# Second input projection in a two-block layer: 46 instead of 34 gate units computed beside the expert gather, and shorter filling steps behind it

## The reference

```python
# first block
z = rmsnorm(x, norm1_g) @ w_in
merged = gates[:, :, 0] * conformer_conv(conv_in) + gates[:, :, 1] * (windowed_gqa(q, k, v) @ attn_w_o)
x = x + merged @ w_out
x = x + peer_ffn(rmsnorm(x, norm2_g))
x = rmsnorm(x, final_g)
# peer_ffn, per token: 8 heads x 16 experts
u, vv = expert_u[expert_idx], expert_v[expert_idx]
out = sum(gate * gelu(u . h) * vv)
# second block
p = rms_norm(x, norm_g) @ w_in_2
y_a = rwkv7_mix(p_r, p_k, p_v, p_w, p_a) * silu(z_a)
y_b = sliding_window_sink_attn(p_q, p_sk, p_sv) * silu(z_b)
y_c = memory_cross_attn(p_xq, mem) * silu(z_c)
gates = sigmoid(p_gate)          # 3 x 1024 columns
merged = gates[0] * (y_a @ w_proj_a) + gates[1] * (y_b @ w_proj_b) + gates[2] * (y_c @ w_proj_c)
x = x + merged @ w_out
```

## Time and profile before

| | |
|---|---|
| median of three runs | 2453.41 us (2452.80 to 2457.09) |
| the profiled execution | 2445.02 us |
| its span | 2443.2 us |
| TensorE busy in matmuls | 2156.0 us, 88% |
| TensorE weight loads (beside them) | 1428.3 us, 58% |
| VectorE | 1756.2 us, 72% |
| ScalarE | 849.9 us, 35% |
| POOL | 698.8 us, 29% |
| DMA, mean | 291 GB/s |
| TensorE's granted clock | 0.983 of full |

### The profile page before, as it was taken

How to read it: one execution, slowest core, us unless ns; L and a number is a source line. 1 busy time by engine, 2 the same in 40 slices (tenths; PEclk the granted TensorE clock), 3 DMA queues, 4 the chain that set the end, 5 groups by cost and what they waited for, 6 DMA issues and landing times. The chain is left out here.

```text
span 2443.2 us, 34816 instructions
## 1 busy us (share of the span) xinstructions
PE 2156.0 (88%) x12550; PEld 1428.3 (58%) x12550; DVE 1756.2 (72%) x3976; ACT 849.9 (35%) x1966; POOL 698.8 (29%) x580
## 2 busy tenths in 40 slices
PE   8999899998989898877777887789888898999999
PEld 7887566764444444422323333367766788867677
DVE  7999796587767667677777676798887546466763
ACT  4222664243323232223333233433333232225641
POOL 0001312354333333333443333334233000011133
PEclk9999999999999999999999999999999999998999
DMA  4333214599999999999999999999999653232152
GB/s 155 104 104 112 78 53 165 180 395 415 421 420 414 415 419 416 411 416 418 409 420 413 410 419 420 399 413 416 420 398 408 227 188 116 83 126 106 40 194 95
DMA packets 135482, 710.39 MB, mean 291 GB/s; under 512 B 14480, under 2 KB 23568, under 8 KB 69520
## 3 DMA queue, kind: packets, MB, share of 16 engines
q0 software_dynamic: 73728, 536.90, 53.3%
q1 hardware_dynamic: 61584, 171.26, 19.8%
HBM read 686.61 MB, written 21.50 MB: 290 GB/s over the span
## 5 line engine op out<-in xcount | busy, mean ns | idle before, releaser
L2176 PE MATMUL bank<-peer_uv,peer_diag 128*128 128x512 f32 x1856 | 875.3, 614 | 221.9 <-ACT peer_diag L1549 211.1
L1915 DVE SCALAR_TENSOR_TENSOR peer_uv<-peer_uv,h 128x1024 f32<-128x1024 f32 x512 | 618.5, 1219 | 323.8 <-DMA peer_uv<-in_peer_uv,peer_index 321.8
L1596 POOL DMA_INDIRECT peer_uv<-in_peer_uv,peer_index x512 | 536.5, 1048 | 858.6 <-PE bank L2176 599.4
L2176 PEld LDWEIGHTS bank<-peer_uv,peer_diag 128*128 128x128 f32 x1856 | 339.9, 193 | 664.2 <-issue 663.8
L168 PE MATMUL bank<-hT_high,weight_low 128*128 128x512 f32 (+1 forms) x952 | 348.4, 366 | 0.0
L166 PE MATMUL bank<-hT_high,weight_high 128*128 128x512 f32 (+1 forms) x768 | 333.9, 435 | 8.1 <-PEq L454 2.4
L240 POOL TENSOR_TENSOR weight_low<-weight_ring,weight_high 128x1024 fp32r<-128x1024 f32 x52 | 127.4, 2451 | 613.3 <-ACT weight_high L223 613.3
L167 PE MATMUL bank<-hT_low,weight_high 128*128 128x512 f32 (+1 forms) x768 | 285.3, 371 | 1.2 <-issue 1.2
L1542 ACT ACTIVATE peer_gelu<-peer_dots 128x2 f32<-128x2 f32 (+1 forms) x257 | 52.0, 202 | 646.4 <-DVE peer_uv L1915 646.0
L223 ACT ACTIVATE weight_high<-weight_ring 128x1024 fp32r<-128x1024 f32 x148 | 156.2, 1055 | 307.0 <-PE bank L168 297.6
L1549 ACT ACTIVATE peer_diag<-const,peer_weight 128x128 f32<-128x128 f32 x464 | 163.7, 395 | 226.3 <-DVE peer_weight L1711 223.6
(11 more groups left out here) (468 smaller groups left out, 3141.6 us busy)
## 6 DMA issues: line engine op xcount, KB each, us to landing
weight_ring<-in_weights SPq DMA_DIRECT2D x218, 512.0 KB
z_store<-fill_stage SPq DMA_DIRECT2D x36, 256.0 KB, 2.3
peer_uv<-in_peer_uv,peer_index POOLq DMA_INDIRECT x512, 11.8
z_store<-early_stage SPq DMA_DIRECT2D x34, 192.0 KB
merge_z<-z_store SPq DMA_DIRECT2D x8, 768.0 KB, 6.8
merge_z<-z_store SPq DMA_DIRECT2D x12, 512.0 KB, 4.7
raw_query<-in_weights SPq DMA_DIRECT2D x10, 512.0 KB, 6.7
raw_out<-in_weights SPq DMA_DIRECT2D x8, 512.0 KB, 7.0
```

The costliest lines, as they stand in the source:

```text
L1596: pool.indirect_dma_start(uv[:, p % SLOTS], None, peer_uv, bass.IndirectOffsetOnAxis(index[:, n % 2, p % TOPK:p % TOPK + 1], 0)).then_inc( ...
L1915: nc.vector.scalar_tensor_tensor(uv[:, p % SLOTS, 0:D], uv[:, p % SLOTS, 0:D], 1.0, h2[:, t], ALU.mult, ALU.mult, accum_out=dots[:, p % TO ...
L2176: mm = nc.tensor.matmul(bank[2 * t + c][:], diag[:, p % SLOTS], uv[:, p % SLOTS, D + c * 512:D + (c + 1) * 512], start=(n == first_of(t) a ...
```

## The change

`EARLY` goes from 34 to 46, so all gate units are computed beside the gather for 384 tokens. The units begin three groups sooner (group 204 instead of 207), for which the norm of a complete tile is drawn together from 16 groups to 12: its last step on VectorE stood 15 groups after `FINISH_AT`, now 12, and TensorE's turn stood at 9, now at 6. Two instead of three units are left behind the last group, and the copy behind the warm-up Sqrt falls away. A third buffer for the copies lies in the place of a score table. The wait for all stores moves from the end of SP's program in this block to ScalarE's in `rwkv_prepare`. VectorE may make two low parts in one group. Behind the gather all fill steps are short ones now, 46 x 4 = 184, and the blocks from the chain of states on hold fewer: 7 instead of 14 in the chain, 12 instead of 24 in the outputs (the 3 steps behind the last output become 1), 11 instead of 18 in the finishing block, 18 instead of 38 in the windowed attention, none instead of 2 in the merge. Up to the end of the solve they are 136, as before.

```diff
@@ constants
-EARLY = 34
+EARLY = 46
+STAGES = 3
@@ class Weights
+        self.early_stored = [ctx.enter_context(nc.semaphore(f"early_stored{i}")) for i in range(STAGES)]
...
+    def wait_early_stored(self, eng):
+
+        for i in range(STAGES):
+            eng.wait_ge(self.early_stored[i], 16 * ((EARLY + STAGES - 1 - i) // STAGES))
@@ places beside the gather
-FINISH_DVE = (2, 4, 6, 8, 9, 12, 13, 14, 15)
-FINISH_ACT = (3, 5, 7, 10, 11, 12, 13)
-FINISH_PE = 9
+FINISH_DVE = (2, 3, 4, 5, 6, 9, 10, 11, 12)
+FINISH_ACT = (2, 3, 4, 7, 8, 9, 10)
+FINISH_PE = 6
...
-Z_FROM = FINISH_AT[2] + 15
+Z_FROM = FINISH_AT[2] + 12
...
-Z_AFTER = 3
+Z_AFTER = 2
@@ merge_and_experts, buffers
-        sc = [same_place(nc, "peer_sc0", [P, 2, 2, NKEYS], z_offset + 24 * 1024), st.sb("sc1", [P, 2, 2, NKEYS])]
+        sc1, sc1_offset = placed(nc, st.ctx, "peer_sc1", [P, 2, 2, NKEYS])
+        sc = [same_place(nc, "peer_sc0", [P, 2, 2, NKEYS], z_offset + 24 * 1024), sc1]
...
-        early_stage = same_place(nc, "early_stage", [P, 2, EARLY_T], attnT.high_offset)
+        early_stage = [same_place(nc, f"early_stage{i}", [P, EARLY_T], offset) for i, offset in enumerate(
+            (attnT.high_offset, attnT.high_offset + 4 * EARLY_T, sc1_offset))]
@@ merge_and_experts, SP
-                    sp.dma_start(early_store[n][:, 0:EARLY_T], early_stage[:, n % 2]).then_inc(early_stored[n % 2], 16)
+                    sp.dma_start(early_store[n][:, 0:EARLY_T], early_stage[n % STAGES][:]).then_inc(w.early_stored[n % STAGES], 16)
...
                 sp.wait_ge(kv_stored, 16)
-                for i in range(2):
-                    sp.wait_ge(early_stored[i], 16 * ((EARLY + 1 - i) // 2))
@@ merge_and_experts, ScalarE
-                        to = early_stage[:, e % 2]
-                        if e >= 2:
-                            act.wait_ge(early_stored[e % 2], 16 * (e // 2))
+                        to = early_stage[e % STAGES][:]
+                        if e >= STAGES:
+                            act.wait_ge(w.early_stored[e % STAGES], 16 * (e // STAGES))
...
                 nc.scalar.activation(warm[:, 1:2], warm[:, 0:1], ACT.Sqrt)
-                keep_z(EARLY_UNITS - 3)
                 next(norming[TT - 1])
@@ merge_and_experts, VectorE
-                    if lows < LOWS_BESIDE and low_group(lows) <= g:
+                    while lows < LOWS_BESIDE and low_group(lows) <= g:
@@ rwkv_prepare, ScalarE, behind the two high parts of the last tokens' h
+                w.wait_early_stored(act)
@@ rwkv_core, TensorE
-                    fill.pe(pe, 2)
+                    fill.pe(pe, 1)
                     fill.mark()
                     if ch:
                         carry(ch)
...
-                    fill.pe(pe, 6 if t + 1 < TT else 3)
+                    fill.pe(pe, 3 if t + 1 < TT else 2)
...
-                fill.pe(pe, 3)
+                fill.pe(pe, 1)
@@ finish_branches, TensorE
-                fill.pe(pe, 8)
+                fill.pe(pe, 4)
...
-                fill.pe(pe, 7)
+                fill.pe(pe, 4)
```

More of the change, by code:

```diff
@@ L1227, in merge_and_experts @@
         z_kept, last_act, last_dve = (st.sem(n) for n in ("z_kept", "last_act", "last_dve"))
-        early_stored = [st.sem(f"early_stored{i}") for i in range(2)]
         vector_added = st.sem("vector_added")
```

2 lines of the change are left out of this document (1 added, 1 removed).

## The result

The changed kernel takes 2461.9 us in the median of eight runs (2458.5 to 2468.2), the kernel before, beside it, 2453.1 (2450.1 to 2457.1): a ratio of 1.0037, 95% interval 1.0022 to 1.0052. The forecast was 2436.

The account below looks back on a forecast made before the run. The prediction took the gather as bound by bytes (DMA full) and TensorE's queue with its fill steps as lengthening the path behind it. 17 - 6.5 - 28 = -17.5 gave 2436 us against the median, range 2424 to 2451.

Parts of the forecast that it names:

- term 5: Behind the gather: fewer, shorter fill steps free 53 us of TensorE at most; -28 us claimed, kept between -20 and -35.
- terms 1 and 2: Gather: bytes of twelve more units, 20.9 us, less 4 us given back by the third stage buffer; +17 us together.
- Twelve more units: Gather: 8.65 MB more at 414 GB/s, nothing hiding them, TensorE still fitting; 20.9 us.
- The third buffer: Gather: nearly all of ScalarE's waits for stores go, giving back 4 us; ends 0 and 9.
- Norms together: Gather: a tile's norm steps in five groups instead of eight cost zero; ends 0 and +4.
- The chain behind the last group: From last gelu to next block: squares start sooner, shorter wait at the block's end; -6.5 us, ends -3 and -8.
- Attention: Windowed attention: fill from 38 whole to 18 short steps; -7 us, ends -4 and -13.
- Outputs: Outputs behind the chain of states: fill from 24 whole to 12 short steps; -11 us, ends -4 and -13.
- Chain: Chain of states: fill from 7 x 2 whole to 7 x 1 short steps; -5 us, ends -2 and -7.
- Finishing block: Finishing block: fill from 18 whole to 11 short steps; -3.5 us, ends 0 and -9.
- The fourth rival: Windowed attention: its last ten rounds, without fill, run at half clock, 8 us more, 2444 us; chance 5%.
- The slower rival: Gather turns from bytes to engines as TensorE's idle time stays: +49 instead of +17, 2468 us; chance 9%.

Follow-up runs that it names:

- early40_dense: early40b with its same 51 units put into 45 groups instead of 50; 2456.3 us, ratio 1.0012.
- less_pe: The change with only the first of three matmuls in each step of the 46 gate units, low-part products left out; 2461.9 us in one run.
- defer_high: The change with the second high part of a double group put off to behind the next gelu; 2465.9 us, ratio 1.0046.
- best34: early34 with the norms over 16 groups and the units from group 207, as before the change; 2443.1 us, ratio 0.9947.
- early34: The change with EARLY back at 34 and the fill steps of before; 2444.5 us, ratio 0.9966.
- stages2: The change with two stage buffers instead of three; 2481.9 us, ratio 1.0105.
- warm: The change with additional unread 128-column matmuls in finishing block and windowed attention, and attention fill steps one in each of 17 rounds; 2466.5 us, ratio 1.0053.
- att1: The change with one short fill step in each of 18 rounds of the windowed attention instead of two in each of 9; 2463.0 us, ratio 1.0038.
- less_both: less_pe with, in addition, VectorE adding no pick of the last tile, TensorE summing all; 2468.7 us in one run.
- nofill: The change with no fill step in chain, outputs and windowed attention, those 37 short steps moved to the merge; 2474.6 us, ratio 1.0084.
- early40b: The change with EARLY at 40, its fill steps up to the finishing block, then 7, the rest nearly all whole in attention and merge; 2445.5 us, ratio 0.9962.
- e34_warm: early34 with 24 additional unread 128-column matmuls ahead of the wait for swz in the finishing block; 2446.1 us, ratio 0.9968.

## Why the forecast was wrong, point by point

The sum was -17.5 and the medians show +8.8, so 26.3 us are missing. About 20 of them lie in term 5, the shorter fill steps, and 8 in terms 1 and 2, the gather (+17 forecast, +24.8 measured against the mean of the two profiles of before); the chain gave 1 us more than forecast.

1. **Twelve more units: the bytes were right.** 20.9 us were forecast. The first six cost 7.8 to 11 us (1922.1 and 1923.1 against 1914.3 and 1911.9), 10.4 by bytes; the next six would cost the same, and cost 18. The failed step is that I weighed each engine's work in a mean group ("TensorE still fits, with 0.45 us to spare") and so priced the units by their bytes alone. 9.12 steps in a group, with eight steps to a unit, means two units in each seventh group. Their copies, stores, loads and low parts stand in one group, with gelu and diagonal of the next queued behind them, and once in a while the exponentials of the next pair too. `early40_dense` measured 9.6 us for six such groups. Which wait within them costs most stays open: `less_pe` and `defer_high` each took one thing away, and the long groups stayed or moved.
2. **The third buffer was mis-sized:** 4 us back, ends 0 and 9; measured, by taking the buffer out, 8 at 34 units and 20 at 46. (Against the kernel before, `best34` has the third buffer with 34 units and ends the gather 3 to 4 us sooner, with one unit more inside: there the forecast size holds. It was at 46 units that it did not.) What I wrote of it, that the waits are no loss while DMA stays full, was the error: they cost rate, 405 against 418 GB/s over 300 us, at DMA shares (1.00 and 1.02) that look full either way. The estimate from the Trainium skill (DMA: Bandwidth & Descriptors, Anatomy of one DMA), a store home in 2.45 us, is not borne out: a store took 10.8 us to land in the changed kernel, by the median of its page of the profile. That section of the Trainium skill fits its figures to transfers that GpSimd issues; this store is issued by SP.
3. **Norms together: nothing,** as forecast, with three buffers.
4. **The chain behind the last group: right.** -6.5 forecast, -7.4 measured (21.9 to 14.5; 22.6 in the second profile of before), 13.8 in `early34`. TensorE's wait at the block's end fell by 3.2 us where I had 1.8.
5. **Fill steps: the step that failed most.** Forecast -28; measured -1.5 against the first profile of before, -7 against the second. From the 13 units to the end, six profiles with the fill steps of before take 505.7 to 521.6 us, 515.2 on the mean; seven with about the change's steps (the change, `stages2`, `warm`, `less_pe`, `att1`, `defer_high`, `less_both`) 500.4 to 510.7, 505.6 on the mean. Only the two lowest of the six are the kernel before itself, 508.4 on the mean; the other four have 34 units and the rest of the change. So these steps are worth 3 to 10 us, in a stretch that varies by as much. The medians leave 8 us for them: +8.8 is +24.8 for the gather, -7.7 for the chain and -8.3 for all behind. What failed is how much of the 53 us saved on TensorE I let through, 28: the blocks' own pieces take over sooner than I reckoned, and in the finishing block, by the estimate in point 6, the lower clock takes what was saved.
   - Attention, -7: "past that its own pieces and ScalarE's exponentials set the pace" was right, and I should have read its length from it. With 38 whole steps of 0.79 us, 30 us of TensorE, the attention took 5.8 us more than with none (56.4 against 50.6), so those were nearly free. The change's 18 short ones cost 6.4: the first three rounds take 11.8 us where they took 6.2, at half clock and with the 3.19 us wait for a fill bank.
   - Outputs, -11, measured -6.6: the floor is 26.2, near my 25.3, but the 12 short steps lie on top of it with 3.5 us.
   - Chain, -5, measured -0.9 (-2.2 against the second profile): 15.2 without any fill, at a granted clock of 0.87.
   - Finishing block, -3.5, measured +1.2 and -1.3 against the two profiles. Here TensorE is busy nearly throughout behind the product with swz, and the length goes with the granted clock. Kernels with the same steps in this block took 53.0 us at 0.69 (`stages2`), 49.3 at 0.74 (the change), 48.0 at 0.78 (`less_pe`), 45.5 at 0.81 (`less_both`); and, with the steps of before, 56.5 at 0.73 (`best34`), 51.6 at 0.80 (`early34`), 48.1 at 0.82 (before). `nofill` is out of line with 44.9 at 0.77. Why the clock differs between these runs is not shown.
   - Merge and what stands in front of it, -1.5, measured +0.5 and -1.0; the memory attention in it lost 1.5 to the clock (point 6).
   - The stage of the 13 units and the solve, forecast 0, grew by 3.7 us: TensorE stood 3.25 us at 2158, beside a read of 1 MB, and ran at half clock behind it. `stages2`, `warm` and `att1` took 208.6, 208.7 and 208.3 us for this stage too, `nofill` 204.8; the cause was not tested.
6. **The clock.** The fourth rival came true as a fact: 0.74, 0.83 and 0.88 where 0.82, 1.00 and 1.00 stood. I had given it 5%, because the memory attention shows 1.00 without fill; but its clock goes with the attention in front of it, 1.00 in `warm` and `early40b` (1.00 and 0.97 there), 0.88 in the change; not strictly, since the four kernels with 34 units show 0.92 or 0.93 behind an attention at 1.00. In the attention of the change the clock is 0.50 from 2260 to 2270, after TensorE was busy 2.15 us of the 5 before. The Trainium skill (TensorE: Matmul & The Clock Gate, HAM oscillation), by which idle gaps between matmuls throttle the array again, agrees with that; the finishing block of `e34_warm`, where the clock fell behind 15 us without idle time, is not explained by gaps. The price was 1.5 us in the memory attention (28.1 us from its first matmul to the first of the next product, 26.5 before). In the finishing block it was more, by an estimate: what a clock below full takes from a busy TensorE is (1 - 0.74) x 49.3 = 12.8 us in the change, and (1 - 0.82) x 48.1 = 8.7 before. The 4 us between them are as much as the shorter steps were to save there. I had this rival's price in the attention alone.
7. **The slower rival,** engines instead of bytes, had the right sign and the wrong engine. Its mark, a pace above 7.2 us a group, holds from group 223 to 247 (7.2 to 7.65), as means over eight groups, but TensorE relieved of a quarter of its work gave back 3 us only.

What the profile of before could have told: the earlier trace rows give the pace, the wait on ScalarE, and the table of groups, written out, the groups that get two copies.

## What to carry to other kernels

When side work is laid into a loop by a table, count its pieces in the fullest iteration, not the mean: just above one piece an iteration, one iteration in seven here held two, and those were the long ones, the more so where other rare work fell into the same iteration. Before shortening filler work, find what the stretch takes with none of it; only what exceeds that floor can be gained, and where TensorE is the busy engine, the clock it is granted counts as much as its steps. And a buffer that ends a wait may be worth far more than the transfer share shows, but the next wait in the same queue is already there.

## What the runs showed of the hardware

- A DMA share of 1.00 to 1.02 covers rates from 401 to 418 GB/s in the same stage: full by share is not full by bytes.
- In the changed kernel a 192 KB store lands 11.1 us after its issue from 1600 to 1940 us (median), a 512 KB load 8.2 there and 4.1 over the whole kernel. The load that ScalarE waited for until 1746.30 had been issued at 1733.05.
- The granted clock stood at 0.50 through a whole stretch in which TensorE showed busy: two windows in the finishing block of the changed kernel,

```profile
2225.00:2230.00 5.00, 5.00 (x26) 5.00 (x25) 0.00 (x0) 0.00 (x0) 0.00 (x0) 0.50 0.00 0
2230.00:2235.00 5.00, 5.00 (x12) 2.98 (x13) 1.55 (x3) 0.00 (x0) 0.00 (x0) 0.50 0.00 0
```

  TensorE had been busy 2.19 of 5 us from 2210 to 2215 and 4.17 from 2215 to 2220. In `e34_warm` it had been busy 15 of 15 us, and the clock fell to 0.50 all the same.
- Ten executions of one kernel spread over 18 us (`early40_dense`, 2447.2 to 2465.4).
